# High and low parts of the split activations stored alternately in one buffer each, in a transformer block with three-pass matmuls

## The chip, the cores and the metric

The kernel runs on one core of one Trainium2 chip. The metric is device time in microseconds; the median of three runs of the kernel before is 1105.91 us (1105.87 to 1106.67).

## The reference, cut to what matters

One layer of a streaming encoder block over 256 tokens of width 2048, all in float32:

```python
h = rms_norm(x, norm1_w)
p = h @ w_in                       # 2048 x 6152: mLSTM q,k,v,o, gates, attention q,k,v
y = concat(mlstm(p...), diff_attention(p...))
x = x + y @ w_out                  # 2048 x 2048
h = rms_norm(x, norm2_w)
x = x + (silu(h @ w_gate) * (h @ w_up)) @ w_down   # 2048 x 5632 twice, 5632 x 2048
```

The five large products hold nearly all the arithmetic. The rest (a causal convolution, a chunked recurrence with a running maximum, two softmax maps per head) is small beside them.

## The kernel before, in words

Every large product is a sum of three matmuls on operands of type fp32r (32-bit floats as TensorE takes them for these matmuls). An operand X is split into a high part (X written out as fp32r) and a low part (X minus the high part, written out as fp32r). The product is high x low + low x high + high x high, added up in PSUM.

The weights come from HBM in chunks of 128 x 1024 floats into a ring of 8 raw buffers (`w_raw`). For each step of a plan, ScalarE copies a chunk to `w_hi` (L845), VectorE subtracts to get `w_lo` (L1143), and TensorE waits for that (`lo_done`) and runs 12 matmuls on it, or 3 or 6 in the parts of a "pair" step. `w_hi` and `w_lo` are rings of 4 buffers. Within each product the weights are the moving operand, 512 columns wide, and the activations the stationary one: a tile of 128 features x 128 tokens. `chunk` (L480, L482, L483) and `three` (L702 to L704) issue the three matmuls; each of them loads its stationary tile anew, in a weight load of its own (an LDWEIGHTS row of the profile, engine PEld), which runs beside the matmul in front.

The activations are split the same way and stay in SBUF: `act_hi` and `act_lo` (16 tiles of 128 x 256, first for the normalised input, then for that of the feed-forward part, last for sums of hidden tiles), `y_hi` and `y_lo` for the output of the mixer, `hid_hi` and `hid_lo` for the hidden layer (44 tiles; the last four first hold sums, `sum_hi` and `sum_lo`), and the small `third_hi` and `third_lo`. The sums serve a Strassen-like scheme in the "pair" steps, in which seven products stand for eight (VectorE makes the weights' sums in place, L1154 to L1160).

Who writes these buffers: ScalarE makes the high part and VectorE the low part, at the start in 16 instructions of 256 elements each (L858 and L1055, L1188 and L1435), later in instructions of 512 or 1024 elements: L850 and L1182 (`turned_hi`, `weighted_lo`), L965 and L1316 (y), L1031 and L1426 (hidden, 22 each), L1116 and L1547 (sums). VectorE also reads both parts of the hidden tiles back, to add them (L1536). Besides the stationary tiles, one place of TensorE reads the buffers as the moving operand: `gates` (L504, L505), 32 matmuls of 256 columns, after chunk 10.

The order of the work is written out by hand: each engine has one program, with small work put between the splits of given chunks (`small_work`, `ff_slice`), and counting semaphores between the engines. In a slice of the feed-forward part, ScalarE and VectorE split the hidden tiles of the slice before after step 4.

Stretches of the span: input projection with mixer to about 320 us, output projection to about 412 us, eleven feed-forward slices to about 870 us, the down projection to the end.

Of the kernel before, what the change touches and what calls it, by code (L numbers as in the profile page):

```python
# [28 lines left out]
F32 = mybir.dt.float32  # L29
F32R = mybir.dt.float32r  # L30
ALU = mybir.AluOpType
ACT = mybir.ActivationFunctionType
# [3 lines left out]
SEQ = 256  # L36
TT = SEQ // P
D = 2048
KT = D // P
D_FF = 5632  # L40
KF = D_FF // P
NG = 512
CH = 2 * NG
# [40 lines left out]
SUM_BLOCKS = (slice(4, 6), slice(6, 8), slice(3, 9, 5), slice(1, 3))  # L84
# [72 lines left out]
def hybrid_block_kernel(nc, x, x_turned, params, gate_bias, gate_w, weights, out):  # L157
    ctx = ExitStack()
    with ctx:
        def sb(name, shape, dt=F32, stack=ctx, parts=P):  # L160
            return stack.enter_context(nc.sbuf_tensor(name, [parts] + shape, dt))

        def sem(name):
            return ctx.enter_context(nc.semaphore(name))


        res = sb("res", [TT, D])
        act_hi = sb("act_hi", [KT, SEQ], F32R)
        act_lo = sb("act_lo", [KT, SEQ], F32R)
        w_raw = sb("w_raw", [RAW, CH])  # L170
        w_hi = sb("w_hi", [SPLIT, CH], F32R)
        w_lo = sb("w_lo", [SPLIT, CH], F32R)
# [2 lines left out]
        gated = sb("gated", [TT, NG])  # L175
# [43 lines left out]
        start.close()  # L219

        mix = ExitStack()
        y_hi = sb("y_hi", [KT, SEQ], F32R, mix)
        y_lo = sb("y_lo", [KT, SEQ], F32R, mix)
        mv = sb("mv", [TT, HEADS, DV + 1], F32, mix)
        probs = sb("probs", [2, P + SEQ], F32, mix)
        a_tmp = sb("a_tmp", [P + SEQ], F32, mix)
# [36 lines left out]
        lstm.close()  # L263
        mix.close()
        ff = ExitStack()
        hid_hi = sb("hid_hi", [KF, SEQ], F32R, ff)
        hid_lo = sb("hid_lo", [KF, SEQ], F32R, ff)
        third_hi = sb("third_hi", [NG], F32R, ff)
        third_lo = sb("third_lo", [NG], F32R, ff)
        sum_hi = hid_hi[:, KF - 4:KF, :].rearrange("p k s -> p (k s)")  # L270
        sum_lo = hid_lo[:, KF - 4:KF, :].rearrange("p k s -> p (k s)")
        down_hi = act_hi[:].rearrange("p k s -> p (k s)")
        down_lo = act_lo[:].rearrange("p k s -> p (k s)")
        ff.close()

        acc = [ctx.enter_context(nc.psum_tensor(f"acc{i}", [P, NG], F32)) for i in range(4)]
# [15 lines left out]
        third_hi_done = sem("third_hi_done")  # L292
# [166 lines left out]
        parts = (slice(0, P), slice(P, P + SEQ))  # L459
# [364 lines left out]
        def _(act):  # L824
# [8 lines left out]
            def split_hi(n):  # L833

                st = PLAN[n]
                src, cols = st.load + (st.part in (1, 3)), slice(0, NG if st.kind == "pair" and st.part == 0 else CH)
                if st.part == 2:
                    act.wait_ge(t13_ready, st.pair + 1)
                elif st.part == 3:
                    act.wait_ge(t4_ready, st.pair + 1)  # L840
                else:
                    act.wait_ge(raw_landed[src % RAW], 16 * (src // RAW + 1))
                if n >= SPLIT:
                    act.wait_ge(chunk_used, n - (SPLIT - 1))
                act.activation(w_hi[:, n % SPLIT, cols], w_raw[:, src % RAW, cols], ACT.Copy).then_inc(hi_done, 1)  # L845
# [170 lines left out]
            def x1_squares(g):  # L1016
                act.wait_ge(x1_ready, 2 * g + 2)
                for t in range(TT):
                    s = act.activation(gated[:, t, :], res[:, t, NG * g:NG * (g + 1)], ACT.Square,
                                       accum_out=ss_x1[:, t, g:g + 1])  # L1020
                s.then_inc(x1_squared, 1)

            def x1_hi(g):
                for t in range(TT):
                    turned_hi(act_hi[:, 4 * g:4 * g + 4, P * t:P * (t + 1)], 5 + 2 * g + t, t)
# [8 lines left out]
            def first_gate():  # L1034

                act.wait_ge(chunk_used, FF0 + GC)
                if N_PAIRS == 3:
                    act.wait_ge(third_lo_done, 1)
                for t in range(TT):
                    act.activation(gated[:, t, :], acc[t][:], ACT.Silu, scale=r2[:, t:t + 1]).then_inc(gate_act, 1)  # L1040
# [31 lines left out]
            def first_slice():  # L1072
                for c in range(FF_CHUNKS):
                    split_hi(FF0 + c)
                    if c == LAG + 2 and N_PAIRS == 3:
                        act.wait_ge(third_step, 4)
                        act.activation(third_hi[:], gated[:, 1, :], ACT.Copy).then_inc(third_hi_done, 1)
                    if c == LAG - 1:
                        x1_squares(3)
                    if c == 2 * LAG:  # L1080
                        x1_hi(3)
                        act.wait_ge(x1_tot, 1)
                        act.activation(root, tot, ACT.Sqrt, bias=eps, scale=1.0 / D).then_inc(x1_root, 1)
                    if c == GC + LAG - 1:
                        act.wait_ge(r2_ready, 1)
                        first_gate()
                    if c == GC + LAG:
                        act.wait_ge(e_summed, 1)
                        act.activation(sum_hi, stage[:].rearrange("p a n -> p (a n)"),
                                       ACT.Copy).then_inc(e_hi_done, 1)  # L1090
# [16 lines left out]
            for n in range(DOWN_START[0], len(PLAN)):  # L1107
# [4 lines left out]
                if c - 2 in SUM_AT and DOWN_PAIRS[0]:  # L1112
                    g = SUM_AT.index(c - 2)
# [14 lines left out]
        def _(dve):  # L1128
# [332 lines left out]
            def first_slice():  # L1461
                turned_x = scaled[:].rearrange("p t (j h s) -> p t j h s", j=2, h=2)
                e = stage[:].rearrange("p a (e j s) -> p (a e) j s", e=2, j=2)
                third = gated[:, 0, :].rearrange("p (h t s) -> p h t s", h=2, t=2)
                third_e = gated[:, 1, :].rearrange("p (e s) -> p e s", e=4)
                for c in range(FF_CHUNKS):
                    split_lo(FF0 + c)
                    if c == LAG - 1:
                        x1_group(3)
                    if c == LAG and N_PAIRS == 3:  # L1470
                        dve.wait_ge(x1_squared, 4)
                        dve.wait_ge(turn_lo, 10)
                        dve.tensor_tensor(gated[:, 0, :], act_hi[:, 10:12, :].bitcast(F32).rearrange("p k s -> p (k s)"),
                                          act_lo[:, 10:12, :].bitcast(F32).rearrange("p k s -> p (k s)"),
                                          ALU.add).then_inc(third_full, 1)
                        dve.wait_ge(third_full, 1)
                        block_sums([[third[:, h, t, :] for t in range(TT)] for h in range(2)],
                                   [third_e[:, m, :] for m in range(4)], third_step, 0).then_inc(third_step, 1)
                    if c == LAG + 3 and N_PAIRS == 3:
                        dve.wait_ge(third_hi_done, 1)  # L1480
                        dve.tensor_tensor(third_lo[:], gated[:, 1, :], third_hi[:].bitcast(F32),
                                          ALU.subtract).then_inc(third_lo_done, 1)
                    if c == 2 * LAG:
                        x1_block(3)
                        dve.wait_ge(x1_squared, 4)
                        dve.tensor_reduce(tot, ss_x1, AX.X, ALU.add).then_inc(x1_tot, 1)
                        dve.wait_ge(x1_root, 1)
                        dve.reciprocal(r2, root).then_inc(r2_ready, 1)
                        dve.wait_ge(r2_ready, 1)
                    if c == GC:  # L1490
                        block_sums([[turned_x[:, t, :, h, :] for t in range(TT)] for h in range(2)],
                                   [e[:, m] for m in range(4)], e_step, 0).then_inc(e_summed, 1)
                    if c == GC + LAG + 1:
                        dve.wait_ge(e_hi_done, 1)
                        dve.tensor_tensor(sum_lo, stage[:].rearrange("p a n -> p (a n)"),
                                          sum_hi.bitcast(F32), ALU.subtract).then_inc(e_lo_done, 1)
                        dve.wait_ge(e_lo_done, 1)
                        for t in range(TT):
                            dve.memset(stage[:, t, :], 0.0).then_inc(evac_step, 1)
# [30 lines left out]
            def hidden_full(g):  # L1530
                if g:
                    dve.wait_ge(down_e_lo, g)
                parts = [h[:].bitcast(F32).rearrange("p (m f) s -> p m (f s)", f=4)[:, SUM_BLOCKS[g], NG:CH]
                         for h in (hid_hi, hid_lo)]
                dve.wait_ge(hid_lo_done, 2 * FF_SLICES - 2)
                dve.tensor_tensor(scaled[:], parts[0], parts[1], ALU.add).then_inc(full_ready, 1)  # L1536
# [119 lines left out]
```

## Time and profile before

| | |
|---|---|
| Median of three runs | 1105.91 us |
| Profiled execution | 1106.12 us, of it span 1104.2 us |
| Instructions | 12990, of them 4951 matmuls with 4951 weight loads |
| Busy: PE, PEld | 1096.4 us (99%), 907.3 us (82%) |
| Busy: DVE, ACT | 854.6 us (77%), 616.2 us (56%) |
| Granted clock of TensorE | 1.0 of full speed |
| HBM | 209.8 MB read, 192 GB/s over the span |

PE is TensorE's matmuls, PEld its weight loads, DVE VectorE, ACT ScalarE. Matmuls are pipelined, so their durations overlap: the distance from one start to the next, called pitch below, says what one costs. A number behind L is a line of the kernel.

### The profile page before, as it was taken

To read this page: it belongs to the slowest core of one execution; us is meant where nothing else is said; L and a number is where in the kernel's file an instruction comes from. 1 tells how busy PE (TensorE), PEld (TensorE's weight loads), DVE (VectorE), ACT (ScalarE), POOL (GpSimd) and SP (SyncE) were. 2 spreads that over 40 slices of the span, in tenths; PEclk is the share of its full clock that TensorE was granted. 3 is DMA by queue.
4 is the path that set the end of the run, shared out by engine and by line. 5 is a ranking of instruction groups with operands and counts; after the bars stand their busy time and mean duration, and the time that the engine had idled before them with its cause. 6 is when DMAs were issued, how large, how long until landed. Compare 5 with 4: busy or idle time off the path is not lost.

```text
span 1104.2 us, 12990 instructions
## 1 busy us (share of the span) xinstructions
PE 1096.4 (99%) x4951; PEld 907.3 (82%) x4951; DVE 854.6 (77%) x1037; ACT 616.2 (56%) x771; POOL 3.3 (0%) x18
## 2 busy tenths in 40 slices
PE   8999999999999999999999999999999999999998
PEld 7888887888888888888888888888888888888887
DVE  5676546764565666898998999999999889878886
ACT  7566466754544445456555555555665545635552
POOL 1000000000000000000000000000000000000000
PEclk9999999999999999999999999999999999999999
DMA  9745544564466565465664664665665755675662
GB/s 354 274 166 184 174 143 139 173 208 154 142 202 188 177 200 183 154 221 182 200 223 166 215 211 164 212 215 178 196 214 193 235 191 172 198 224 180 196 204 104
DMA packets 59909, 212.77 MB, mean 193 GB/s; under 512 B 6728, under 2 KB 6856, under 8 KB 59848
## 3 DMA queue, kind: packets, MB, share of 16 engines
q1 hardware_dynamic: 59552, 211.84, 58.5%
q8 instruction: 39, 0.64, 0.2%
q14 instruction: 22, 0.18, 0.1%
q10 hardware_dynamic: 296, 0.11, 0.0%
HBM read 209.83 MB, written 2.10 MB: 192 GB/s over the span
## 4 chain that ended last, share of the span: by engine, by line
PE 97%; DMA 1%; DVE 1%; ACT 1%; issue 0%; ACTq 0%
PE acc L480 14%; PE acc L483 14%; PE acc L482 14%; PE acc L704 11%; PE acc L702 11%; PE acc L703 11%; PE aux L703 3%; PE aux L702 3%; PE aux L704 3%; PE aux L483 3%; PE aux L482 3%; PE aux L480 3%; PE aux L494 2%; DMA w_raw<-in_weights 1%; DMA par<-in_params 0%; PE aux L544 0%
## 5 line engine op out<-in xcount | busy, mean ns | idle before, releaser
L1143 DVE TENSOR_TENSOR w_lo<-w_raw,w_hi 128x1024 fp32r<-128x1024 f32 (+1 forms) x477 | 545.8, 1172 | 178.2 <-ACT w_hi L845 176.4
L845 ACT ACTIVATE w_hi<-w_raw 128x1024 fp32r<-128x1024 f32 (+1 forms) x477 | 476.5, 1018 | 318.1 <-PE acc L704 90.1
L702 PE MATMUL acc<-w_lo,act_hi 128*128 128x512 f32 x473 | 185.0, 391 | 0.0
L704 PE MATMUL acc<-w_hi,act_hi 128*128 128x512 f32 x473 | 184.2, 389 | 0.0
L703 PE MATMUL acc<-w_hi,act_lo 128*128 128x512 f32 x473 | 184.0, 389 | 0.0
L480 PE MATMUL acc<-w_lo,act_hi 128*128 128x512 f32 x448 | 178.1, 398 | 2.4 <-DVE w_lo L1143 2.4
L483 PE MATMUL acc<-w_hi,act_hi 128*128 128x512 f32 x448 | 174.7, 390 | 0.0
L482 PE MATMUL acc<-w_hi,act_lo 128*128 128x512 f32 x448 | 174.5, 389 | 0.0
L704 PEld LDWEIGHTS acc<-w_hi,act_hi 128*128 128x128 f32 x473 | 88.8, 188 | 18.6
L703 PEld LDWEIGHTS acc<-w_hi,act_lo 128*128 128x128 f32 x473 | 88.8, 188 | 18.2
L702 PEld LDWEIGHTS acc<-w_lo,act_hi 128*128 128x128 f32 x473 | 88.8, 188 | 18.1
L480 PEld LDWEIGHTS acc<-w_lo,act_hi 128*128 128x128 f32 x448 | 84.1, 188 | 21.9 <-issue 4.3
L483 PEld LDWEIGHTS acc<-w_hi,act_hi 128*128 128x128 f32 x448 | 84.1, 188 | 17.8
L482 PEld LDWEIGHTS acc<-w_hi,act_lo 128*128 128x128 f32 x448 | 84.2, 188 | 16.6
L1154 DVE TENSOR_TENSOR w_raw<-w_raw 128x1024 f32<-128x1024 f32 x43 | 52.7, 1225 | 1.5
L480 PE MATMUL acc<-w_lo,y_hi 128*128 128x512 f32 x128 | 50.2, 392 | 0.0
L483 PE MATMUL acc<-w_hi,y_hi 128*128 128x512 f32 x128 | 49.9, 390 | 0.0
L482 PE MATMUL acc<-w_hi,y_lo 128*128 128x512 f32 x128 | 49.8, 389 | 0.0
L480 PE MATMUL acc<-w_lo,hid_hi 128*128 128x512 f32 x124 | 48.3, 390 | 0.0
L483 PE MATMUL aux<-w_hi,hid_hi 128*128 128x512 f32 x124 | 48.2, 389 | 0.0
L480 PE MATMUL aux<-w_lo,hid_hi 128*128 128x512 f32 x124 | 48.2, 389 | 0.0
L483 PE MATMUL acc<-w_hi,hid_hi 128*128 128x512 f32 x124 | 48.2, 389 | 0.0
(275 smaller groups left out, 1274.8 us busy)
## 6 DMA issues: line engine op xcount, KB each, us to landing
w_raw<-in_weights SPq DMA_DIRECT2D x391, 512.0 KB, 4.0
res<-in_x SPq DMA_DIRECT2D x4, 512.0 KB, 11.0
out<-res SPq DMA_DIRECT2D x8, 256.0 KB, 3.3
xt<-in_x_turned SPq DMA_DIRECT2D x3, 512.0 KB, 8.8
xt<-in_x_turned SPq DMA_DIRECT2D x2, 256.0 KB, 3.9
w_raw<-in_weights SPq DMA_DIRECT2D x2, 256.0 KB, 3.8
w_if<-in_gate_w ACTq DMA_DIRECT2D x1, 64.0 KB, 5.5
par<-in_params ACTq DMA_DIRECT2D x1, 47.0 KB, 3.6
```

The costliest lines, as they stand in the source:

```text
L480: pe.matmul(bank[:], hi[:, k, tok], w_lo[:, slot, cols], start=first and kk == 0, stop=False)
L482: pe.matmul(bank[:], lo[:, k, tok], w_hi[:, slot, cols], start=False, stop=False)
L483: mm = pe.matmul(bank[:], hi[:, k, tok], w_hi[:, slot, cols], start=False, stop=last and kk == len(kts) - 1)
L494: mm = pe.transpose(banks[t][:, P * b:P * (b + 1)], src[:, t, P * b:P * (b + 1)], ident[:])
L702: pe.matmul(bank[:], hi, w_lo[:, slot, cols], start=start, stop=False)
L703: pe.matmul(bank[:], lo, w_hi[:, slot, cols], start=False, stop=False)
L704: return pe.matmul(bank[:], hi, w_hi[:, slot, cols], start=False, stop=stop)
L845: act.activation(w_hi[:, n % SPLIT, cols], w_raw[:, src % RAW, cols], ACT.Copy).then_inc(hi_done, 1)
L1143: dve.tensor_tensor(w_lo[:, n % SPLIT, cols], w_raw[:, src % RAW, cols], w_hi[:, n % SPLIT, cols].bitcast(F32), ALU.subtract).then_inc(lo_ ...
L1154: dve.tensor_tensor(b[:, 0:2, :], b[:, 0:4:3, :], b[:, 1:2, :].to_broadcast([P, 2, NG]), ALU.add).then_inc(t13_ready, 1)
```

## The change

Each pair of buffers becomes one buffer with a last axis of 2; high parts are at index 0 and low parts at index 1. The names of before are now views of it, whose neighbouring elements are 8 bytes apart instead of 4. Sizes in sum, addresses of the other buffers, instructions, their order and all waits stay. Every instruction that writes or reads one of the parts now does so in steps of two elements: the writes of ScalarE and VectorE, the reads of VectorE in its subtractions, the stationary tiles of all the three-pass matmuls, and the moving operand of `gates`. The weights' buffers (`w_raw`, `w_hi`, `w_lo`) stay as they were.

```diff
-        act_hi = sb("act_hi", [KT, SEQ], F32R)
-        act_lo = sb("act_lo", [KT, SEQ], F32R)
+        act = sb("act", [KT, SEQ, 2], F32R)
+        act_hi, act_lo = act[:, :, :, 0], act[:, :, :, 1]
...
-        y_hi = sb("y_hi", [KT, SEQ], F32R, mix)
-        y_lo = sb("y_lo", [KT, SEQ], F32R, mix)
+        y_parts = sb("y_parts", [KT, SEQ, 2], F32R, mix)
+        y_hi, y_lo = y_parts[:, :, :, 0], y_parts[:, :, :, 1]
...
-        hid_hi = sb("hid_hi", [KF, SEQ], F32R, ff)
-        hid_lo = sb("hid_lo", [KF, SEQ], F32R, ff)
-        third_hi = sb("third_hi", [NG], F32R, ff)
-        third_lo = sb("third_lo", [NG], F32R, ff)
+        hid = sb("hid", [KF, SEQ, 2], F32R, ff)
+        hid_hi, hid_lo = hid[:, :, :, 0], hid[:, :, :, 1]
+        third = sb("third", [NG, 2], F32R, ff)
+        third_hi, third_lo = third[:, :, 0], third[:, :, 1]
...
-        down_hi = act_hi[:].rearrange("p k s -> p (k s)")
-        down_lo = act_lo[:].rearrange("p k s -> p (k s)")
+        down_hi = act_hi.rearrange("p k s -> p (k s)")
+        down_lo = act_lo.rearrange("p k s -> p (k s)")
```

The other edits only drop a `[:]` behind names that are views now.

## Rows read from the trace of the kernel before

**Rows 1.** The page: busy time of each engine, and the chain that ended last.

```profile
PE 1096.4 (99%) x4951; PEld 907.3 (82%) x4951; DVE 854.6 (77%) x1037; ACT 616.2 (56%) x771; POOL 3.3 (0%) x18
...
PE 97%; DMA 1%; DVE 1%; ACT 1%; issue 0%; ACTq 0%
```

**Rows 2.** Groups by line and shape: count, busy us, mean ns, idle before.

```profile
L480 PE MATMUL acc<-w_lo,act_hi 128*128 128x512 f32 x448 | 178.1, 398 | 2.4 <-DVE w_lo L1143 2.4
L480 PEld LDWEIGHTS acc<-w_lo,act_hi 128*128 128x128 f32 x448 | 84.1, 188 | 21.9 <-issue 4.3 <-DVE w_lo L1143 0.8
L505 PE MATMUL aux<-act_lo,w_if_parts 128*128 128x256 f32 x16 | 3.9, 282 | 0.0
```

**Rows 3.** Timeline of PE late in the down projection: start us, us, instruction.

```profile
1097.84 0.39 PE L483 MATMUL aux<-w_hi,hid_hi 128*128 128x512 f32 x1
...
1100.56 0.39 PE L483 MATMUL aux<-w_hi,hid_hi 128*128 128x512 f32 x1
```

**Rows 4.** Timeline of PE in the mixer stretch and in a feed-forward slice.

```profile
299.64 0.39 PE L480 MATMUL acc<-w_lo,act_hi 128*128 128x512 f32 x1
...
301.91 0.39 PE L482 MATMUL acc<-w_hi,act_lo 128*128 128x512 f32 x1
...
585.80 0.39 PE L703 MATMUL acc<-w_hi,hid_lo 128*128 128x512 f32 x1
...
587.61 0.39 PE L702 MATMUL acc<-w_lo,act_hi 128*128 128x512 f32 x1
...
589.88 0.39 PE L703 MATMUL acc<-w_hi,act_lo 128*128 128x512 f32 x1
```

**Rows 5.** Windows: us, then PE, PEld, DVE, ACT busy, clock, DMA share, GB/s.

```profile
200.00:320.00 120.00, 120.00 (x539) 98.68 (x538) 74.00 (x108) 67.72 (x97) 0.00 (x0) 1.00 0.55 178
...
500.00:600.00 100.00, 100.00 (x450) 82.88 (x450) 91.67 (x100) 57.54 (x64) 0.00 (x0) 1.00 0.61 200
```

**Rows 6.** Timeline of PE in the gates' matmuls, 256 columns each.

```profile
39.85 0.28 PE L504 MATMUL aux<-act_hi,w_if_parts 128*128 128x256 f32 x1
...
41.16 0.28 PE L505 MATMUL aux<-act_lo,w_if_parts 128*128 128x256 f32 x1
```

**Rows 7.** Timeline of the weight loads behind the gates.

```profile
43.78 0.19 PEld L480 LDWEIGHTS acc<-w_lo,act_hi 128*128 128x128 f32 x1
43.89 0.19 PEld L482 LDWEIGHTS acc<-w_hi,act_lo 128*128 128x128 f32 x1
44.13 0.19 PEld L483 LDWEIGHTS acc<-w_hi,act_hi 128*128 128x128 f32 x1
```

**Rows 8.** Groups of ScalarE and VectorE by line and shape.

```profile
L845 ACT ACTIVATE w_hi<-w_raw 128x1024 fp32r<-128x1024 f32 x434 | 449.3, 1056 | 292.0 <-PE aux L483 84.8 <-PE acc L483 81.7 <-PE acc L704 73.5
...
L1143 DVE TENSOR_TENSOR w_lo<-w_raw,w_hi 128x512 fp32r<-128x512 f32 x43 | 29.4, 684 | 1.1 <-ACT w_hi L845 1.1
L845 ACT ACTIVATE w_hi<-w_raw 128x512 fp32r<-128x512 f32 x43 | 27.2, 633 | 26.1 <-PE acc L704 16.6 <-PE aux L704 5.8 <-PE aux L483 3.3
...
L1426 DVE TENSOR_TENSOR hid_lo<-aux,hid_hi 128x512 fp32r<-128x512 f32 x22 | 14.1, 683 | 2.3 <-ACT hid_hi L1031 2.3
...
L1031 ACT ACTIVATE hid_hi<-aux 128x512 fp32r<-128x512 f32 x22 | 12.0, 596 | 26.7 <-PE aux L494 26.7
...
L1188 DVE SCALAR_TENSOR_TENSOR act_lo<-xt,par,act_hi 128x256 fp32r<-128x256 f32 x14 | 5.9, 477 | 0.0
...
L1547 DVE TENSOR_TENSOR act_lo<-gated,act_hi 128x1024 fp32r<-128x1024 f32 x4 | 4.9, 1218 | 0.0
```

**Rows 9.** Timeline of DVE in a feed-forward slice, with idle time in brackets.

```profile
579.22 1.28 DVE L1426 TENSOR_TENSOR hid_lo<-aux,hid_hi 128x512 fp32r<-128x512 f32 x2
...
585.56 4.10 DVE L1143 TENSOR_TENSOR w_lo<-w_raw,w_hi 128x1024 fp32r<-128x1024 f32 x4 [1.16 <-ACT w_hi L845]
```

**Rows 10.** Timeline of all engines at the start.

```profile
16.80 1.67 DVE L1188 SCALAR_TENSOR_TENSOR act_lo<-xt,par,act_hi 128x256 fp32r<-128x256 f32 x4
...
19.32 1.23 DVE L1143 TENSOR_TENSOR w_lo<-w_raw,w_hi 128x1024 fp32r<-128x1024 f32 x1 [0.85 <-ACT w_hi L845]
...
20.69 0.47 PE L480 MATMUL acc<-w_lo,act_hi 128*128 128x512 f32 x1 [0.66 <-DVE w_lo L1143]
```

**Rows 11.** Waits over the span: total us, times, longest.

```profile
DVE w_lo L1143 <- ACT w_hi L845: 176.4, 140, 5.7
...
PE acc L480 <- DVE w_lo L1143: 2.4, 3, 1.2
```

More of the change, by code:

```diff
@@ L1076, in first_slice @@
                         act.wait_ge(third_step, 4)
-                        act.activation(third_hi[:], gated[:, 1, :], ACT.Copy).then_inc(third_hi_done, 1)
+                        act.activation(third_hi, gated[:, 1, :], ACT.Copy).then_inc(third_hi_done, 1)
                     if c == LAG - 1:
@@ L1480, in first_slice @@
                         dve.wait_ge(third_hi_done, 1)
-                        dve.tensor_tensor(third_lo[:], gated[:, 1, :], third_hi[:].bitcast(F32),
+                        dve.tensor_tensor(third_lo, gated[:, 1, :], third_hi.bitcast(F32),
                                           ALU.subtract).then_inc(third_lo_done, 1)
@@ L1532, in hidden_full @@
                     dve.wait_ge(down_e_lo, g)
-                parts = [h[:].bitcast(F32).rearrange("p (m f) s -> p m (f s)", f=4)[:, SUM_BLOCKS[g], NG:CH]
+                parts = [h.bitcast(F32).rearrange("p (m f) s -> p m (f s)", f=4)[:, SUM_BLOCKS[g], NG:CH]
                          for h in (hid_hi, hid_lo)]
```

## The prediction, made before the changed kernel ran

> **What bounds the kernel now.** I read the page's busy times and its chain first, then the timeline of PE for the distance between matmuls, and last the waits and the windows. The page has PE busy for 99% of the span, and 97% of the chain that ended last lies on PE [rows 1]. So the time is the number of matmuls times their pitch. The three-pass matmuls are 4575 of the 4951: the plan has 306 whole steps of 12 and 43 pairs of 3 + 6 + 6 + 6, and 306 x 12 + 43 x 21 = 4575. Their duration of 390 to 398 ns [rows 2] isn't their price, since they overlap. Late in the down projection twelve pitches take 1100.56 - 1097.84 = 2.72 us, 226.7 ns each [rows 3]. It is the same in the middle: ten pitches in 2.27 us (227 ns) in the mixer stretch, where DVE is busy for 62%, and 18 pitches in 4.08 us (226.7 ns) in a feed-forward slice, where DVE is busy for 92% [rows 4, 5]. The clock is granted in full throughout [rows 5]. 4575 x 226.67 ns = 1037 us; the other 67 us of the span are warm-up, transposes, gates, the mixer's small matmuls and a few waits. PE waited for `w_lo` only 2.4 us in all [rows 11], while DVE itself waited 176.4 us for ScalarE [rows 11]: there is cover on DVE almost everywhere.
>
> So the change can be worth something in one place above all: each of the 4575 pitches holds one weight load, and every one of these loads now steps over 8 bytes per element. One nanosecond more or less per pitch is 4.6 us.
>
> **The stationary tiles.** A load lasts 188 ns [rows 2], but that is latency too. Two shorter distances show what a load occupies. Behind the gates two loads of activation tiles start 43.89 - 43.78 = 0.11 us apart [rows 7]. And the gates' own matmuls, of 256 columns with a load of 128 x 128 each, run eleven pitches in 1.31 us, 119 ns each [rows 6]: a load and everything that it holds up fit in 119 ns. Of the 226.7 ns of a main pitch, about 108 ns are therefore free for a longer load. No row shows a strided load, so I bound it. Lower end: nothing changes, 0. Upper end, if reading goes by the stretch of memory passed over and the load was already at its limit: it passes over 1024 bytes instead of 512 and takes 220 ns instead of 110, and the pitch becomes 119 + 110 = 229 ns, 2.3 ns more, + 11 us (with the smallest and largest pitch that the rows allow, 0 to + 15 us). What I take is 0, because the rows show TensorE reading faster: the moving operand, 512 contiguous floats of 4 bytes, goes by in at most 226.7 ns, 2048 bytes at 9.0 bytes per ns, while a load of 512 bytes in 110 ns goes at 4.7. A load in steps of two would pass over 1024 bytes in 110 ns, 9.3 bytes per ns, the pace that the moving side shows already. If the loading side can't keep that pace it still has the 108 ns.
>
> The trace shows no price of a stride, only that contiguous pace. The Trainium skill states one, in "SBUF — State Buffer" (section "Door 1: The DMA port swizzle", the note on cachelines): lines are 16 bytes, and accesses stay at full bandwidth as long as each line is hit at least twice, so that float32 may stride up to 4 elements for free. Steps of 8 bytes hit each line twice, and the sum would be 0 by it. Its page "Advanced Engine Details and Errata" (section "SBUF Cachelines") names a penalty once every access needs another line; that would be reached at 16 bytes, not here.
>
> **The gates.** Their 32 matmuls read the buffers as the moving operand, now over 2048 bytes instead of 1024 in 119 ns, 17 bytes per ns, which no row shows. Lower end 0. Upper end: the pitch doubles, 32 x 119 = + 3.8 us, and all of it is on PE. I take 0, since 4-byte elements are still wanted at the same pace, but the end stays in the range.
>
> **The writes and reads of ScalarE and VectorE.** By the difference between 1024 and 512 elements ScalarE takes (1056 - 633) / 512 = 0.83 ns per element, and VectorE (1218 - 684) / 512 = 1.04 ns [rows 8]; both are per element and not per byte wherever the rows let one see it, and no row has steps of two. Lower end 0, upper end a doubled share per element. What hides each:
> In a slice, `hid_lo` is two instructions of 512 elements (683 ns each) and `hid_hi` two of 596 ns [rows 8]. Doubled, they add 2 x 512 x 1.04 = 1.07 us on DVE and 0.85 us on ACT. Behind them DVE idles 1.16 us before its split for the second half of the pair [rows 9], and this split, ending at 585.56 + 1.22 = 586.8, is used at 587.61 [rows 4], 0.8 us later. Cover 1.16 + 0.8 = 1.96 against at most 1.92 us: 0 in all eleven slices.
> The sums of the down projection (4 x L1536, L1116, L1547) and the y parts (8 of each) are first used several steps after they are made, in stretches where DVE waits for ScalarE and not PE for DVE [rows 11]: 0.
> At the start there is little cover. PE starts step 4 at 20.69 after 0.66 us of idle behind `w_lo` [rows 10], and the 14 + 2 instructions of 256 elements for `act_hi` and `act_lo` stand in the engines' queues ahead of the splits (L1188: four in 1.67 us, [rows 10]). Doubled per element they add 16 x 256 x 0.83 = 3.4 us on ACT and 4.3 us on DVE, mostly side by side, part of it in time in which both wait for DMA. So 0 to + 4 us; I take 0.
>
> **Sum.** 0 on the stationary tiles, 0 on the gates, 0 on the other engines. Instructions, waits, DMAs and queues are the same ones, so nothing is moved past anything. The profiled execution took 1106.12 us, 1104.2 of span and 1.9 around it, and lies 0.2 us above the median of the runs, 1105.91. I predict 1106.0 us. What a measurement of this kernel can tell from no change is about 0.2%, 2.2 us.
>
> **Rivals.**
> *A. The weight load takes reading time from the running matmul.* This is the way to slower that I take most seriously. From the durations of 282 ns for 256 columns and 390 for 512 [rows 2] a column streams in about 0.42 ns, so 512 of them take 216 ns; at the full clock of 2.4 GHz, one column a cycle, 213.3. The pitch is 226.7: 11 to 13 ns are over, and they are there with 256 columns too (119 against 107). If that is the time in which the load's reads push aside those of the moving operand, and if it grows with the bytes passed over, it doubles: 4575 x (11 to 13.3) = + 50 to + 61 us, 1156 to 1167 us. It decides from the first load on, in every stretch alike. For it: the surplus is constant, and the same for 256 and 512 columns. Against it: a handing-over of the tile inside the array would look the same. The Trainium skill speaks against it in "TensorE: Matmul & The Clock Gate" (section "Step-by-step: what each phase is for"): matmul and weight load read SBUF through two independent ports. It doesn't explain the 11 to 13 ns, though, as its own gap for 512 columns is 216 ns.
> *B. The load gets longer than its cover.* Doubled, 1106 to 1121 us, as worked out; if each element cost four times as much, 119 + 330 = 449 ns per pitch, 222 ns more, some 2120 us. It decides from about 108 ns of additional load time. For it: loads run at half the pace of the moving side, which may be a limit of their own. Against it: that pace is per element, and the number of elements stays.
> *C. Only the gates or the start pay.* + 2 to + 8 us together, 1108 to 1114 us.
> *D. Faster.* Nothing gets shorter; at most the surplus of 11 to 13 ns could shrink, if it came from where high and low parts lie relative to each other, which no row suggests. The least that would be told apart is 1103.7 us.
>
> **Chances and range.** No change 0.66; A 0.09; B 0.10, of which 0.07 for the doubled load (half of it under 1114) and 0.03 beyond; C 0.11; D 0.04. Inside 0.2%: the 0.66. Slower by over 0.2%: A, B and C, 0.30. Faster: 0.04. The range from 1103.7 to 1122 us holds no change, C and the doubled load, 0.84; it leaves out A, the rest of B and D.
>
> **What would show it.** On the changed kernel the pitch should still be 226.7 ns in the three places read here, the gates' eleven pitches 1.31 us, the loads 188 ns, `hid_lo` 683 ns, `hid_hi` 596 ns and `act_lo` at the start 477 ns. A shows as a pitch of 238 to 240 ns with loads that may keep their 188 ns; B as loads of about 300 ns with a pitch of 227 to 230; C as a longer stretch between 39.85 and 43.7 us or a later start of step 4. The prediction is wrong if the pitch moves by more than 0.5 ns.

## The result, and the profile after

The changed kernel takes 1138.11 us (1137.96 to 1138.23), the kernel before 1106.1 us on the same chip: a ratio of 1.0287 (95% interval 1.0272 to 1.0302), 32.0 us slower. No change, 1106.0 us with a range up to 1122, was forecast; that was wrong in sign and size.

The page of the changed kernel, busy times and the chain that ended last:

```profile
PE 1128.3 (99%) x4951; PEld 937.4 (83%) x4951; DVE 856.7 (75%) x1037; ACT 617.7 (54%) x771; POOL 3.3 (0%) x18
...
PE 97%; DMA 1%; DVE 1%; ACT 1%; issue 0%; ACTq 0%
```

The same instructions, and PE is still the whole chain [rows 1]. PE is busy 31.9 us longer, DVE and ACT by 2.1 and 1.5 us. PE's share of the span stays at 99%, so the time was lost inside PE and not in waits. The timeline of PE late in the down projection, as in [rows 3]:

```profile
1127.87 0.39 PE L480 MATMUL acc<-w_lo,hid 128*128 128x512 f32 x1
...
1130.67 0.40 PE L480 MATMUL acc<-w_lo,hid 128*128 128x512 f32 x1
```

Twelve pitches take 2.80 us: 233.3 ns each instead of 226.7. At the full clock of 2.4 GHz these are 560 and 544 cycles, for 512 columns. The same holds in the mixer stretch (299.84 to 301.01 us, five pitches in 1.17 us, 234 ns). Now the gates, whose moving operand has become strided, to set beside [rows 6]:

```profile
40.42 0.39 PE L504 MATMUL aux<-act,w_if_parts 128*128 128x256 f32 x1
...
41.79 0.41 PE L504 MATMUL aux<-act,w_if_parts 128*128 128x256 f32 x1
```

Six pitches in 1.37 us: 228 ns instead of 119. From the first to the last of the 32 matmuls the gates take 7.11 instead of 3.69 us. Last, the groups by line and shape, to set beside [rows 2, 8]:

```profile
L480 PEld LDWEIGHTS acc<-w_lo,act 128*128 128x128 f32 x448 | 87.1, 194 | 21.7 <-issue 4.2 <-DVE w_lo L1143 1.2
...
L1143 DVE TENSOR_TENSOR w_lo<-w_raw,w_hi 128x512 fp32r<-128x512 f32 x43 | 29.6, 687 | 1.2 <-ACT w_hi L845 1.1
...
L1426 DVE TENSOR_TENSOR hid<-aux,hid 128x512 fp32r<-128x512 f32 x22 | 14.2, 687 | 4.8 <-ACT hid L1031 4.8
...
L1031 ACT ACTIVATE hid<-aux 128x512 fp32r<-128x512 f32 x22 | 12.7, 635 | 27.6 <-PE aux L494 27.6
...
L1188 DVE SCALAR_TENSOR_TENSOR act<-xt,par,act 128x256 fp32r<-128x256 f32 x14 | 5.9, 480 | 0.0
...
L1547 DVE TENSOR_TENSOR act<-gated,act 128x1024 fp32r<-128x1024 f32 x4 | 4.9, 1220 | 0.0
```

A load lasts 6 ns longer (194 against 188) and ScalarE's `hid_hi` 39 ns. VectorE's instructions last 2 to 4 ns longer, but that isn't the step: its 43 splits of 512 columns of weights (L1143), whose operands did not change, went from 684 to 687 ns too, and a contiguous kernel below (k4_moving_8_on) has 686 ns where `hid_lo` has 687 here. Set stretch by stretch, from the starts of the same matmuls in both traces, the loss is 10.5 us in the input projection and mixer (3.4 of it in the gates), 2.4 in the output projection, 12.8 in the eleven slices and 6.7 in the down projection, less 0.4 us by which the first matmul came earlier: 32.0 us. It is spread like the matmuls.

### The profile page after: what moved, and what is told of

Same layout as the page of the kernel before. It is cut to its first block, busy times and chain, and to the rows that moved or that the text cites. A ratio compares the mean times of both kernels' runs of the same rounds, so it can differ in the third digit from the quotient of the medians.

```text
span 1136.2 us, 12990 instructions
## 1 busy us (share of the span) xinstructions
PE 1128.3 (99%) x4951; PEld 937.4 (83%) x4951; DVE 856.7 (75%) x1037; ACT 617.7 (54%) x771; POOL 3.3 (0%) x18
## 4 chain that ended last, share of the span: by engine, by line
PE 97%; DMA 1%; DVE 1%; ACT 1%; issue 0%; ACTq 0%
PE acc L480 14%; PE acc L483 14%; PE acc L482 14%; PE acc L702 11%; PE acc L703 11%; PE acc L704 11%; PE aux L703 3%; PE aux L704 3%; PE aux L702 3%; PE aux L483 3%; PE aux L482 3%; PE aux L480 3%; PE aux L494 2%; DMA w_raw<-in_weights 1%; DMA par<-in_params 0%; PE aux L504 0%
## 5 line engine op out<-in xcount | busy, mean ns | idle before, releaser
L1143 DVE TENSOR_TENSOR w_lo<-w_raw,w_hi 128x1024 fp32r<-128x1024 f32 (+1 forms) x477 | 546.7, 1173 | 194.6 <-ACT w_hi L845 193.0
L702 PE MATMUL acc<-w_lo,act 128*128 128x512 f32 x473 | 187.4, 396 | 0.0
L703 PE MATMUL acc<-w_hi,act 128*128 128x512 f32 x473 | 186.5, 394 | 0.0
L704 PE MATMUL acc<-w_hi,act 128*128 128x512 f32 x473 | 186.5, 394 | 0.0
L480 PE MATMUL acc<-w_lo,act 128*128 128x512 f32 x448 | 180.7, 403 | 2.7 <-DVE w_lo L1143 2.7
L483 PE MATMUL acc<-w_hi,act 128*128 128x512 f32 x448 | 176.9, 395 | 0.0
L482 PE MATMUL acc<-w_hi,act 128*128 128x512 f32 x448 | 176.8, 395 | 0.0
L704 PEld LDWEIGHTS acc<-w_hi,act 128*128 128x128 f32 x473 | 91.5, 193 | 18.8
L702 PEld LDWEIGHTS acc<-w_lo,act 128*128 128x128 f32 x473 | 91.6, 194 | 18.4
L703 PEld LDWEIGHTS acc<-w_hi,act 128*128 128x128 f32 x473 | 91.6, 194 | 18.4
L480 PEld LDWEIGHTS acc<-w_lo,act 128*128 128x128 f32 x448 | 87.1, 194 | 21.7 <-issue 4.2
L483 PEld LDWEIGHTS acc<-w_hi,act 128*128 128x128 f32 x448 | 87.0, 194 | 17.8
L482 PEld LDWEIGHTS acc<-w_hi,act 128*128 128x128 f32 x448 | 87.0, 194 | 16.3
L480 PE MATMUL acc<-w_lo,y_parts 128*128 128x512 f32 x128 | 50.8, 397 | 0.0
L482 PE MATMUL acc<-w_hi,y_parts 128*128 128x512 f32 x128 | 50.5, 394 | 0.0
L483 PE MATMUL acc<-w_hi,y_parts 128*128 128x512 f32 x128 | 50.5, 394 | 0.0
L480 PE MATMUL acc<-w_lo,hid 128*128 128x512 f32 x124 | 49.0, 395 | 0.0
L483 PE MATMUL aux<-w_hi,hid 128*128 128x512 f32 x124 | 48.9, 394 | 0.0
L483 PE MATMUL acc<-w_hi,hid 128*128 128x512 f32 x124 | 48.9, 394 | 0.0
L482 PE MATMUL acc<-w_hi,hid 128*128 128x512 f32 x124 | 48.9, 394 | 0.0
```

Of the source, the lines that this page charges most:

```text
L480: pe.matmul(bank[:], hi[:, k, tok], w_lo[:, slot, cols], start=first and kk == 0, stop=False)
L482: pe.matmul(bank[:], lo[:, k, tok], w_hi[:, slot, cols], start=False, stop=False)
L483: mm = pe.matmul(bank[:], hi[:, k, tok], w_hi[:, slot, cols], start=False, stop=last and kk == len(kts) - 1)
L702: pe.matmul(bank[:], hi, w_lo[:, slot, cols], start=start, stop=False)
L703: pe.matmul(bank[:], lo, w_hi[:, slot, cols], start=False, stop=False)
L704: return pe.matmul(bank[:], hi, w_hi[:, slot, cols], start=False, stop=stop)
```

## The experiments

### Which buffers, and is it the sharing or the step?

Two kernels each make one part of the change alone; a third one lets high and low parts share a buffer but alternate tile by tile, with 256 contiguous elements each.

```diff
 k1_hid_only, against the changed kernel (act and y as before)
-        act = sb("act", [KT, SEQ, 2], F32R)
-        act_hi, act_lo = act[:, :, :, 0], act[:, :, :, 1]
+        act_hi = sb("act_hi", [KT, SEQ], F32R)[:]
+        act_lo = sb("act_lo", [KT, SEQ], F32R)[:]
...
 k2_act_y_only, against the changed kernel (hid and third as before)
-        hid = sb("hid", [KF, SEQ, 2], F32R, ff)
-        hid_hi, hid_lo = hid[:, :, :, 0], hid[:, :, :, 1]
+        hid_hi = sb("hid_hi", [KF, SEQ], F32R, ff)[:]
+        hid_lo = sb("hid_lo", [KF, SEQ], F32R, ff)[:]
...
 k3_tile_by_tile, against the changed kernel (y, hid and third alike)
-        act = sb("act", [KT, SEQ, 2], F32R)
-        act_hi, act_lo = act[:, :, :, 0], act[:, :, :, 1]
+        act = sb("act", [KT, 2, SEQ], F32R)
+        act_hi, act_lo = act[:, :, 0, :], act[:, :, 1, :]
```

> Only the hidden parts and the small third sums alternate element by element; act and y parts are as before. 734 + 367 + 120 = 1221 of the 4575 three-pass matmuls load strided tiles. Main theory (the pitch of each matmul with a strided stationary tile rises by 6.67 ns, wherever it stands): 1221 x 6.67 ns = + 8.1 us, 1114.2 us, pitch 233.3 in the down projection and 226.7 in the input projection, gates at 119 ns. Rival (ScalarE's and VectorE's strided writes and reads carry the loss through waits): little of it in the down projection's plain steps, so under + 3 us, or a loss that shows as gaps of PE and not in the pitch.

Measured: 1114.30 us, 1.0076 of before (1.0061 to 1.0091), + 8.3 us.

> Only the act and y parts alternate element by element; the hidden parts are as before. 2970 + 384 = 3354 matmuls load strided tiles, and the gates' 32 matmuls read a strided moving operand. Main theory: 3354 x 6.67 ns = + 22.4 us, and 31 pitches of the gates x 110 ns = + 3.4 us, together + 25.8 us, 1131.9 us; with the hidden parts' 8.1 us the sum is 33.9, against 32.0 us measured for the whole change. Rival (loss through waits): pitch unchanged and gaps.

Measured: 1130.19 us, 1.0219 (1.0202 to 1.0236), + 24.2 us, 1.7 less than expected. The two parts add up to 32.5 us, against 32.0 for the whole. In its trace the down projection's plain steps with hidden tiles run at about 227 ns a pitch and the steps with act or y tiles at about 233.3.

> High and low parts share one buffer as in the changed kernel, but alternate tile by tile, 256 contiguous elements of one and then of the other. Main theory (only the 8-byte step costs): pitch 226.7, gates 119 ns, 1106.1 us, within 0.2%. Rival (sharing a buffer, or high and low parts lying near each other, costs by conflicts between writers and readers): slower than before by up to the 32 us of the changed kernel, with a pitch above 226.7.

Measured: 1106.07 us, 1.0001 (0.9992 to 1.0010). So neither sharing a buffer nor lying side by side costs anything; the step of 8 bytes does, and it costs by the number of matmuls that load such tiles. The rival of waits falls in all three.

### What the step costs by itself

Three kernels leave the block out and hold only series of matmuls back to back, one series per line. Some of the first one's lines (`steps(t, s, n, j)` takes n elements s apart):

```python
 71  pe.matmul(o(i), st[:, 128 * (i % 2) + 0:...], mv[:, 512 * (i // 3 % 2) + 0:...], **f(i))   # plain
 74  pe.matmul(o(i), steps(st, 2, 128, i % 2, 0, 1), mv[...], **f(i))                           # stationary 2
101  pe.matmul(o(i, 128, 384), steps(st, 2, 128, i % 2, 0, 1), mv[...], **f(i))                 # 384 columns
110  pe.matmul(o(i, 32, 512), st[:, 32 * (i % 2) + 0:...], mv[...], **f(i))                     # 32 weights
116  pe.matmul(o(i), st[...], steps(mv, 2, 512, i // 3 % 2, 0, 1), **f(i))                      # moving 2
```

> The kernel holds nothing of the block but series of 48 matmuls back to back, one series per line: type fp32r, 128 weights, 512 columns unless the line says otherwise, its output is the input passed through. The changed kernel's pitch rose from 226.7 to 233.3 ns, 16 cycles at 2.4 GHz, and the surplus over 512 columns (213.3 ns) from 13.3 to 20.0 ns. Theory 1 (collision): the reads of a weight load push aside those of the running matmul, more of them with a stride. Then the surplus goes with the number of weights: with 64 weights 220.0 ns plain and 223.3 with stride 2, with 32 weights 216.7 and 218.3; and with a moving operand that runs at half pace, where there is room between its reads, the surplus falls to a few ns. Theory 2 (hand-over): a fixed last part of each load can't be hidden, and the stride makes that part 6.7 ns longer, as the load's own duration rose from 188 to 194 ns. Then 64 and 32 weights give 226.7 and 233.3 ns too, and 384 columns give 173.3 and 180.0. Both expect plain 226.7 and stationary stride 2 233.3. Stationary strides 3, 4, 8, 16: if the unit of reading is 16 bytes, a step between 2 and 4; if it is 8 bytes, nothing more after 2. Moving stride 2: 440 ns (the gates' 256 columns went from 119 to 229 ns). bf16: no surplus to speak of at stride 1, 216 ns.

The timeline of PE, one piece per series (start us, us). The pitch is the distance to the next series' start, divided by its 48 matmuls; lines left out lie between the pieces.

```profile
43.10 11.05 PE L71 MATMUL bank<-mv,st 128*128 128x512 f32 x48
53.98 11.36 PE L74 MATMUL bank<-mv,st 128*128 128x512 f32 x48
65.18 11.46 PE L77 MATMUL bank<-mv,st 128*128 128x512 f32 x48
...
110.83 5.91 PE L89 MATMUL bank<-mv,st 128*128 128x256 f32 x48
116.57 5.92 PE L92 MATMUL bank<-mv,st 128*128 128x256 f32 x48
122.33 11.37 PE L95 MATMUL bank<-mv,st 128*128 128x256 f32 x48
133.53 8.52 PE L98 MATMUL bank<-mv,st 128*128 128x384 f32 x48
141.89 8.48 PE L101 MATMUL bank<-mv,st 128*128 128x384 f32 x48
150.21 11.20 PE L104 MATMUL bank<-mv,st 128*64 128x512 f32 x48
...
172.33 11.20 PE L110 MATMUL bank<-mv,st 128*32 128x512 f32 x48
183.37 11.37 PE L113 MATMUL bank<-mv,st 128*32 128x512 f32 x48
194.57 21.82 PE L116 MATMUL bank<-mv,st 128*128 128x512 f32 x48
216.21 21.99 PE L119 MATMUL bank<-mv,st 128*128 128x512 f32 x48
...
368.99 10.52 PE L149 MATMUL bank<-mv,st 128*128 128x512 bf16 x47
379.35 10.52 PE L152 MATMUL bank<-mv,st 128*128 128x512 bf16 x47
```

Plain: 10.88 us / 48 = 226.7 ns; stationary stride 2: 11.20 / 48 = 233.3. Both numbers of the block kernel come out with nothing else running, so it is no contention with other engines or DMA. Strides 3, 4, 8 and 16 give 235, 235, 245 and 235 ns.

The series with 256 columns tell how long the load itself is. Plain they take 5.74 / 48 = 119.6 ns (L89), with a stationary stride of 2 5.76 / 48 = 120.0 ns (L92), so a load in steps of two still fits in 120 ns. With stride 4 they take 11.20 / 48 = 233.3 ns (L95): there the load alone sets the pitch, and it may do so at 512 columns too for the strides from 4 on. What stride 2 costs is something else.

Against both theories, at 384 columns stride 2 costs nothing (L101: 8.32 / 48 = 173.3 ns, 384 + 32 cycles, plain 174), and 32 plain weights are not cheaper than 128 but dearer (L110: 11.04 / 48 = 230.0; L104, 64 weights: 11.03 / 48 = 229.8). The 32-weight tiles start 32 elements apart, which by the next kernel costs something of its own; those of 64 weights start 64 apart and don't have this flaw. So the surplus is neither a number of displaced reads nor a fixed last part of the load. A moving operand with stride 2 takes 451 ns (L116), twice as long. With bf16 and a stationary stride of 2 (L149) the pitch is 10.36 / 48 = 215.8 ns, as with bf16 plain and with stride 4. With float32, in which each matmul leaves two records, it is 429.3 ns per record, plain and with stride 2: 6 cycles over 1024. Of the contiguous types only fp32r, whose moving operand brings 4 bytes a cycle, has the surplus of 32 cycles and its growth with a stationary stride. A bf16 moving operand with stride 2, which passes over the same 2048 bytes, has nearly as much: 10.85 / 48 = 226.0 ns (L155), 542 cycles.

The pitches of plain and stride 2, which repeat to a nanosecond, lie 16 cycles apart (544, 560); those with 64 and 32 weights wander from matmul to matmul around 552. That looked like two streams of reads falling in and out of step, so the second kernel varied widths and start addresses.

> As the first series kernel: nothing of the block, series of 36 matmuls of type fp32r back to back, the output is the input passed through. The first kernel gave a pitch of columns + 32 cycles for plain tiles (544, 416 and 288 cycles at 512, 384 and 256 columns), the same for stride 2 at 384 and 256 columns, but 560 at 512; and 552 with 64 or 32 weights, so that the surplus doesn't go with the number of weights. bf16 and float32 have a surplus of 6 cycles. Theory 3 (phase): two streams of reads, the load's and the moving operand's, meet in the same places of memory in a pattern that depends on where each starts and how it steps; the pitch settles where the pattern repeats. Then start offsets of 2 to 64 elements of either operand change the pitch, at some offsets below 544 or 560 cycles, and stride 2 gives other surpluses at other widths. Theory 4 (volume): a load with stride 2 has a fixed extra cost of 16 cycles that shows only where the moving operand lasts longer than the load. Then 448, 480, 496, 504 and 508 columns all give columns + 32 plain and columns + 48 with stride 2, whatever the offset, and 320 stays like 256 and 384 at + 32. The plain series with 126 to 16 weights tell whether the 552 cycles come with any number but 128; 64 and 32 rows whether the surplus goes with the rows read: 544 either way if it is a matter of the order of reads in each row.

Its timeline, 36 matmuls a series ("4 elements on" means that each tile of that operand starts 4 elements later in its buffer): L68 plain; the stationary operand 4 (L122), 8 (L125) and 64 (L134) elements further on; the moving one 8 (L161), 16 (L164) and 64 (L170) on; 126 weights (L191).

```profile
25.50 8.32 PE L68 MATMUL bank<-mv,st 128*128 128x512 f32 x36
33.66 4.47 PE L71 MATMUL bank<-mv,st 128*128 128x256 f32 x36
...
152.97 8.56 PE L122 MATMUL bank<-mv,st 128*128 128x512 f32 x36
161.37 8.56 PE L125 MATMUL bank<-mv,st 128*128 128x512 f32 x36
...
186.53 8.33 PE L134 MATMUL bank<-mv,st 128*128 128x512 f32 x36
194.70 8.50 PE L137 MATMUL bank<-mv,st 128*128 128x512 f32 x36
...
219.81 8.45 PE L146 MATMUL bank<-mv,st 128*128 128x512 f32 x36
228.09 8.50 PE L149 MATMUL bank<-mv,st 128*128 128x512 f32 x36
...
261.55 8.56 PE L161 MATMUL bank<-mv,st 128*128 128x512 f32 x36
269.95 8.41 PE L164 MATMUL bank<-mv,st 128*128 128x512 f32 x36
278.20 8.53 PE L167 MATMUL bank<-mv,st 128*128 128x512 f32 x36
286.57 8.35 PE L170 MATMUL bank<-mv,st 128*128 128x512 f32 x36
294.75 8.60 PE L173 MATMUL bank<-mv,st 128*128 128x512 f32 x36
...
345.10 8.56 PE L191 MATMUL bank<-mv,st 128*126 128x512 f32 x36
353.49 8.56 PE L194 MATMUL bank<-mv,st 128*120 128x512 f32 x36
```

Contiguous operands cost as much as strided ones once they start in the wrong place: 8.40 / 36 = 233.3 ns with the stationary operand 4 elements on, the same with the moving one 8 on, 229.2 with it 16 on, and 8.17 or 8.18 / 36 = 227 with either 64 on (256 bytes). Even 126 weights instead of 128 give 233. The widths contradict the theory of a fixed cost as well: 504 columns take 544 cycles with stride 1 and with stride 2, 448 take 496 plain and 488 with stride 2. Stride 2 at 512 columns has no start among those tried with the 544 cycles of plain; the stationary operand 16 on gives 552 (L146: 8.28 / 36 = 230.0), the others 555 to 562. That some starts would go below 544 cycles, as theory 3 had it, did not come true.

> As the second series kernel (series of 36 fp32r matmuls, output passed through), with more start offsets. Theory 3 (phase) after the second kernel: the pitch is set by where the two streams start relative to each other. If only the relative start counts, series with both operands 4, 8 or 16 elements on give 544 cycles as plain does, stationary 16 with moving 8 gives what stationary 8 alone does (560), and stationary 128 or 192 on give 544. If the absolute start counts, both on by 8 gives something else than 544. Stationary tiles 132 to 160 apart and moving tiles 516 to 544 apart mix offsets and lie between 544 and 560. No series under 544 is expected at 512 columns; if one is, it would make the kernel before faster: each cycle is 4575 x 0.417 ns = 1.9 us there. Rival: the offsets measured so far changed the pitch by chance of the sequence, and the same offsets give other pitches here.

Some pieces of the third kernel's timeline: both operands 4 (L71), 8 (L74) and 16 (L77) elements on, the stationary one 60 on (L104):

```profile
33.81 8.45 PE L71 MATMUL bank<-mv,st 128*128 128x512 f32 x36
42.09 8.38 PE L74 MATMUL bank<-mv,st 128*128 128x512 f32 x36
50.30 8.35 PE L77 MATMUL bank<-mv,st 128*128 128x512 f32 x36
58.49 8.56 PE L80 MATMUL bank<-mv,st 128*128 128x512 f32 x36
...
125.35 8.33 PE L104 MATMUL bank<-mv,st 128*128 128x512 f32 x36
133.52 8.53 PE L107 MATMUL bank<-mv,st 128*128 128x512 f32 x36
```

They bear theory 3 out in part. Both operands 8 or 16 on give 228.1 and 227.5 ns, against 233.3 for the stationary one alone, so it is mostly the relative start that counts, but not only: both 4 on give 230.0, and the stationary operand 60 on gives 226.9, while the moving one 4 on in the second kernel, the same relative start in a grid of 64, has 231.7. Stride 2 with the moving operand 48 on repeats the 230.0 of the stationary one 16 on. No series at 512 columns is below 544 cycles.

### The same in the block kernel

The four kernels differ in one or two lines that move the weights' buffers against all stationary tiles:

```diff
 k4_moving_8_on, against the kernel before (k6_moving_64_on: 64, k7_moving_16_on: 16)
+        sb("shift", [8])
         w_raw = sb("w_raw", [RAW, CH])
...
-        sb("line_pad", [24 + 96])
+        sb("line_pad", [24 + 96 - 8])
 k5_alternate_48_on, against the changed kernel
+        sb("shift", [48])
         w_raw = sb("w_raw", [RAW, CH])
...
-        sb("line_pad", [24 + 96])
+        sb("line_pad", [24 + 96 + 16])
```

> The kernel before, with all high and low parts contiguous as they were, and 8 unused elements (32 bytes) put ahead of the weights' buffers and taken from the padding behind them, so that the moving operand starts 8 elements further on relative to every stationary tile. Theory 3 (phase): the series with the moving operand 8 elements on had a pitch of 233.3 ns instead of 226.7; 4575 x 6.6 ns = 30.2 us, of which the start and the mixer's waits swallow about 2 us, as they did in the changed kernel: 1134.5 us (1133 to 1137), with no step of two anywhere and the gates still at 119 ns. Rival (the stride itself makes the load longer): 1106 us.

Measured: 1134.02 us, 1.0253 (1.0238 to 1.0268). Everything is contiguous, and the kernel is as slow as with the change, save for the gates. Its timeline of PE and its loads:

```profile
1120.98 0.39 PE L481 MATMUL acc<-w_lo,hid_hi 128*128 128x512 f32 x1
...
1123.78 0.39 PE L481 MATMUL acc<-w_lo,hid_hi 128*128 128x512 f32 x1
```

```profile
L481 PEld LDWEIGHTS acc<-w_lo,act_hi 128*128 128x128 f32 x448 | 84.4, 188 | 23.9 <-issue 3.2 <-DVE w_lo L1144 1.2
...
L506 PE MATMUL aux<-act_lo,w_if_parts 128*128 128x256 f32 x16 | 3.8, 282 | 0.0
```

Twelve pitches in 2.80 us, 233.3 ns, with loads of 188 ns: a pitch of 233.3 ns needs no longer load. The gates stay at 282 ns a matmul and 119 ns a pitch.

> The changed kernel, with the weights' buffers moved on by 48 elements and the padding behind them lengthened by 16, so that act, y and hidden parts start 16 elements after the weights in the grid of 64. Theory 3 (phase): the series with stride 2 and the stationary operand 16 elements on had a pitch of 230.0 ns instead of 233.3: 4575 x 3.3 ns = 15.3 us less than the changed kernel, 1122.8 us (1121 to 1126). Rival (the stride costs a fixed 6.7 ns wherever it starts): 1138.1 us.

Measured: 1125.92 us, 1.0179 (1.0162 to 1.0196): 12.2 us less than the changed kernel, at the slow end of the expected 1121 to 1126. Ten pitches late in its down projection take 2.30 us, 230 ns:

```profile
1112.32 0.39 PE L481 MATMUL acc<-w_lo,hid 128*128 128x512 f32 x1
...
1114.62 0.39 PE L483 MATMUL aux<-w_hi,hid 128*128 128x512 f32 x1
```

Its loads last 195 ns, no shorter than in the changed kernel. A fixed price of the stride is out.

> As the kernel before with the weights' buffers 8 elements further on, but 64 instead of 8. Theory 3 (phase in a grid of 64 elements, 256 bytes): the series with either operand 64 elements on kept 226.7 ns, so 1106.0 us, within 0.2%. Rival (moving the buffers costs something of its own, whatever the distance): about 1134 us as with 8.

Measured: 1106.17 us, 1.0000 (0.9990 to 1.0009).

> The same with 16 elements. The series with the moving operand 16 on had 229.0 ns and the one with the stationary operand 48 on, the same relative start, 228.9: 4575 x 2.3 ns = 10.5 us more, 1116.5 us (1114 to 1119), between the 1106 of 64 elements and the 1134 of 8. Rival (any misalignment costs the same): 1134 us.

Measured: 1114.77 us, 1.0074 (1.0059 to 1.0089), + 8.7 us for 10.5 expected. In its trace ten pitches from 299.61 to 301.90 us take 2.29 us, 229 ns:

```profile
299.61 0.39 PE L481 MATMUL acc<-w_lo,act_hi 128*128 128x512 f32 x1
...
301.90 0.39 PE L483 MATMUL acc<-w_hi,act_lo 128*128 128x512 f32 x1
```

The series predict the block kernel to 3 us: 0, 2.5 and 6.6 ns a pitch, times 4575, are 0, 11.4 and 30.2 us, and + 0.1, + 8.7 and + 27.9 us were measured (the expectation counted with 229.0 ns for 16 elements, its series has 229.2). No arrangement tried beats the kernel before, whose weights and activation tiles all start a multiple of 64 elements apart.

## Why the prediction was wrong

**What bounds the kernel: right.** PE with 4575 three-pass matmuls and their pitch; one nanosecond is 4.6 us.

**The stationary tiles: wrong, and this is the step that failed.** It took 0, with an upper end of + 15 us, because a load fits in 119 ns and a pitch of 226.7 had 108 ns to spare. The spare time was real (with 256 columns the strided load still fits in 120 ns), but the pitch isn't the longer of two durations. It is 512 columns plus a surplus, 32 cycles at best, and the surplus depends on the start addresses, the step and the width of both operands. The step of 8 bytes turned 32 cycles into 48. 4575 x 6.67 ns = 30.5 us, plus 3.4 in the gates, is 33.9. Most of the 1.9 us that are missing is there because the pitches of before weren't all 226.7: over all neighbouring three-pass matmuls under 245 ns apart the mean went from 227.0 to 233.4 ns, so by 6.4. The Trainium skill's rule in "SBUF — State Buffer" (section "Door 1: The DMA port swizzle"), by which float32 may stride up to 4 elements for free, doesn't hold for these 4-byte elements in fp32r: 226.7 became 233.3 ns for a step of two in the stationary operand and 451 in the moving one. In float32 proper the stationary step was free (429.3 ns per record), and a moving one was not run.

**The gates: the upper end came true.** Bound at + 3.8 us, taken as 0, measured 3.4: 31 pitches from 119 to 229 ns. What failed is the sentence that 4-byte elements would be wanted at the same pace. In the series a moving operand in steps of two takes 1082 cycles for 512 columns, about two cycles an element, where a contiguous one takes one.

**ScalarE and VectorE: right.** `hid_lo` + 4 ns and `act_lo` + 3 ns, which come without the step too, and `hid_hi` + 39 ns; ScalarE's part of the rise (39 ns for 512 elements, 0.08 ns each) is far from the doubled share that was the upper end. In the slice DVE's idle before the split came to 1.26 us, against 1.16 [rows 9].

**The rivals.** A had 0.09 and was nearest: slower from the first matmul on, in all stretches, with the surplus as the thing that grows, and even the loads that hardly lengthen. Its size was wrong, 238 to 240 ns for 233.3, since it took the surplus to grow with the bytes passed over; that 64 weights have no less surplus than 128 excludes it in this form. Its counter-argument from the Trainium skill, two independent read ports in "TensorE: Matmul & The Clock Gate" (section "Step-by-step: what each phase is for"), doesn't settle it here: whatever the ports are, where the stationary tile starts changes the matmul's pace (226.7 to 233.3 ns with 4 elements). B fell: doubled loads would have made the 256-column matmuls of the series 220 ns apart, and they stayed at 120. C came true in the gates alone. The range failed because the surplus of 11 to 13 ns, the only number in the trace that nothing explained, was put into a rival instead of into the bounds.

**What stays open.** That the two streams of reads meet in parts of the memory is inferred from the addresses, from the absence of the effect in contiguous bf16 and float32, and from the steady pitches 16 cycles apart. No row shows such a meeting. Nor is it known why both operands 4 elements on, or 126 weights, leave the 544 cycles, or what the 32 cycles of the best case are.

## What to carry to other kernels

For fp32r matmuls of 512 columns, keep both operands contiguous and start every tile of both on one grid of 64 elements (256 bytes), counted here from the first tile: 32 bytes of shift between them cost 2.5%, and interleaving 2.9%. Shifting both alike is not always as good (both 4 elements on: 230.0 ns). Never let an fp32r moving operand step: two elements halve its pace. If parts must share a buffer, alternate them by tiles, which cost nothing (1.0001).

When a pitch is constant to a nanosecond and above the number of columns, ask what makes the difference before calling something beside it hidden; a series of matmuls back to back shows in one run what changes it.

## What the runs showed of the hardware that was not expected

- fp32r, 512 columns: 544 cycles a matmul at best, against 518 in bf16; 384, 320 and 256 columns take 416, 352 and 288 cycles, columns + 32.
- Fewer weights are no cheaper: 128 weights 226.7 ns, 126 and 120 weights 233, 64 and 32 weights 230.
- A load in steps of two fits in 120 ns as a contiguous one does (the pitch at 256 columns), one in steps of four doesn't (233.3 ns). The duration in its record says little: at a stationary stride of 4 the mean is 310 ns and at 8 it is 330, for pitches of 235 and 245 ns.
- A bf16 moving operand with stride 2 costs little (the median pitch goes from 216 to 226 ns), with stride 4 it doubles (451 ns).
- In the series with 32 rows of the array in use the granted clock fell. In the second kernel's windows it is 1.00 over the series with 64 rows, and 0.60 over the one with 32 rows that follows; why was not tested (columns: us, PE, PEld, ACT, POOL busy, clock, DMA share, GB/s):

```profile
395.00:409.00 14.00, 14.00 (x39) 10.29 (x38) 0.00 (x0) 0.00 (x0) 0.60 0.00 1
386.00:395.00 9.00, 9.00 (x40) 6.74 (x38) 0.00 (x0) 0.00 (x0) 1.00 0.00 0
```
